# Two transformer-like blocks on one core: another order of work around dots, latent norm and copies in a selection stage, of depthwise taps, of doubled keys and of first down jobs

## The reference, cut to what matters

```
# block 1
h = rms_norm(x) * (1 + scale) + shift
glu, q, k, v, o, gates, merge = split(h @ w_in)
conv branch:  causal depthwise conv of glu, 31 taps, layer norm, pointwise product
mLSTM branch: short conv of q and k, 4 heads of 256, chunks of 64
x += g1 * (g_conv * y_conv + g_mlstm * y_mlstm) @ w_out
x += g2 * (silu(gate) * up) @ w_ffn_down
# block 2, layer a
q, c_kv, k_rope, q_idx, k_idx, w_idx, q_mem = split(rmsnorm(x) @ a_w_in)
score[t, s] = sum over 16 heads of relu(q_idx[t] . k_idx[s]) * w_idx[t]     # the indexer, heads of 64
keep the 128 highest scores of each row (top-k), attention of 8 heads over the kept
keys, with k and v from rmsnorm(c_kv) through w_uk and w_uv; cross attention to a memory
x += out @ w_out;  x += conv_glu_ffn(rmsnorm(x))                            # ffn1
# block 2, layer b
q, k, v, q_mem = split(rmsnorm(x) @ b_w_in)
banded attention, 16 query heads on 4 key heads of 64, window 128, a sink per head; memory
x += out @ w_out;  x += conv_glu_ffn(rmsnorm(x))                            # ffn2
out = rmsnorm(x)
```

## Time and profile before

| | |
|---|---|
| median of 3 executions | 2098.21 us (2096.07 to 2098.29) |
| the profiled execution | 2093.14 us |
| its span | 2091.3 us |
| granted TensorE clock | 0.999 of full speed |
| PE busy | 2058.3 us (98%) |
| DVE, ACT, POOL busy | 989.1, 885.9, 840.8 us |
| DMA | 220.15 MB, mean 105 GB/s |

### The profile page before, as it was taken

The page is one execution under the profiler, slowest core; times in us unless marked ns, Lnnn a source line. Parts: engine busy times, 40 slices in busy tenths (PEclk is TensorE's granted clock), DMA queues, the critical chain, the costliest instruction groups (busy, mean ns, idle before and its releaser), DMA issues.

```text
span 2091.3 us, 28597 instructions
## 1 busy us (share of the span) xinstructions
PE 2058.3 (98%) x10618; PEld 1735.0 (83%) x10618; DVE 989.1 (47%) x1909; ACT 885.9 (42%) x1307; POOL 840.8 (40%) x273
## 2 busy tenths in 40 slices
PE   9999999999999999999999999999999999999998
PEld 6888877788888888876878888888887688888887
DVE  4889688573411011376985344034323934431432
ACT  3355445363443122534366453233423954432332
POOL 3443432444344444443713443444443044444443
PEclk9999999999999999999999999999999999999999
DMA  9654311235233342332202433333432034324322
GB/s 370 244 183 127 102 61 61 90 98 181 67 103 92 101 118 79 97 108 66 79 24 64 113 100 89 112 102 97 143 86 74 2 96 120 101 79 122 101 73 88
DMA packets 304071, 220.15 MB, mean 105 GB/s; under 512 B 13584, under 2 KB 288144, under 8 KB 301680
## 3 DMA queue, kind: packets, MB, share of 16 engines
q1 hardware_dynamic: 293216, 195.67, 31.4%
q10 hardware_dynamic: 10768, 23.33, 3.7%
HBM read 213.48 MB, written 2.10 MB: 103 GB/s over the span
## 4 chain that ended last, share of the span: by engine, by line
PE 82%; DVE 10%; issue 4%; ACT 3%; POOL 2%; ACTq 0%; DVEq 0%; POOLq 0%
PE bank L912 68%; PE bank L1135 2%; PE bank L1347 2%; DVE bank L2287 2%; PE bank L1325 2%; DVE arena L2784 1%; PE bank L1283 1%; DVE small L2782 1%; DVE bank L2250 1%; PE bank L1334 1%; PE bank L1430 1%; PE bank L1183 1%; DVE bank L2229 1%; POOL w_split_out L2824 1%; ACT w_split L1585 1%
## 5 line engine op out<-in xcount | busy, mean ns | idle before, releaser
L912 PE MATMUL bank<-h_hi,w_split 128*128 128x512 f32 x3696 | 1118.2, 381 | 1.8 <-DVE arena L2652 1.1
L2824 POOL TENSOR_TENSOR w_split<-wslots,w_split 128x2048 fp32r<-128x2048 f32 (+3 forms) x174 | 712.8, 4097 | 987.6 <-ACT w_split L1585 549.5
L912 PEld LDWEIGHTS bank<-h_hi,w_split 128*128 128x128 f32 x3696 | 697.9, 189 | 116.5 <-issue 15.7
L912 PE MATMUL bank<-h_lo,w_split 128*128 128x512 f32 x1848 | 701.1, 379 | 0.0
L912 PEld LDWEIGHTS bank<-h_lo,w_split 128*128 128x128 f32 x1848 | 349.3, 189 | 51.1 <-issue 3.4
L912 PE MATMUL bank<-hid_hi,w_split 128*128 128x512 f32 x1056 | 315.9, 379 | 1.9 <-DVE hid_lo L2532 1.9
L1606 ACT ACTIVATE w_split<-wslots 128x2048 fp32r<-128x2048 f32 (+2 forms) x80 | 141.4, 1767 | 368.0 <-PE bank L912 368.0
L1585 ACT ACTIVATE w_split<-wslots 128x2048 fp32r<-128x2048 f32 (+3 forms) x91 | 158.7, 1744 | 298.6 <-PE bank L912 277.0
L912 PEld LDWEIGHTS bank<-hid_hi,w_split 128*128 128x128 f32 x1056 | 199.6, 189 | 31.4 <-DVE hid_lo L2532 3.2
L912 PE MATMUL bank<-hid_lo,w_split 128*128 128x512 f32 x528 | 200.1, 379 | 0.0
L2250 DVE SCALAR_TENSOR_TENSOR bank<-arena,cols,bank 128x512 f32<-128x512 f32 x240 | 161.4, 750 | 5.5 <-ACT bank L1699 4.9
(11 more groups left out here) (341 smaller groups left out, 2353.5 us busy)
## 6 DMA issues: line engine op xcount, KB each, us to landing
wslots<-in_f_w_up SPq DMA_DIRECT2D x88, 512.0 KB, 4.7
wslots<-in_w_in SPq DMA_DIRECT2D x24, 1024.0 KB, 5.4
wslots<-in_w_ffn_up SPq DMA_DIRECT2D x44, 512.0 KB, 4.6
arena<-in_w_ada ACTq DMA_DIRECT2D x8, 2048.0 KB, 9.6
wslots<-in_f_w_down SPq DMA_DIRECT2D x16, 768.0 KB, 4.9
wslots<-in_a_w_in SPq DMA_DIRECT2D x10, 1024.0 KB, 5.3
wslots<-in_f_w_down SPq DMA_DIRECT2D x16, 640.0 KB, 4.6
arena<-in_w_ada_first SPq DMA_DIRECT2D x8, 1024.0 KB, 18.7
```

The lines of the kernel that those rows point to most:

```text
L912: return nc.tensor.matmul(bank[:], w, woven(x), start=start, stop=stop)
L2824: last = nc.gpsimd.tensor_tensor(part[:, 1, cols_of], slot(p, 1, size)[:, 0, cols_of], part[:, 0, cols_of].bitcast(F32), ALU.subtract)
```

## The change

There are five places, and in all of them the computation stays as it is; only order, banks and the shape of some copies differ.

1. `CONV_TAPS`: five and five taps at steps 14 and 15 become none and ten.
2. Selection stage, PE: `turn_w_idx` moves from a_idx0 to behind product 16 of a_idx1, into bank 6, and waits for `rope_ready` 2; twelve instead of ten pairs stand in a_idx2 and a_idx3, each 7 to 8 products apart; `LATE_DOTS` 14; a_qmem holds two places of dots instead of three, and the latent's mean behind its product 22; the spread moves into a_q0, to bank 5, and a_q0 waits for the root only. ACT and DVE follow: other ranges of relus and weighted sums, ACT's split for a_qmem's successor a_q0 and the latent's squares between the last relus, and its copies of the latent's high part behind a_q0, `latent_norm` from (1, 4) to (2, 0), `memory_queries` from (1, 7) to (1, 10), and each of `ROPES_AT` one round later. POOL lowers a_q1 in one piece instead of four, and the latent's low part behind a_q2.
3. `first_downs`: the first two jobs of `ffn1_down1` and `ffn2_down1` run as tiles 0 to 8 of the first, 0 to 2 of the second, 9 of the first, 3 to 9 of the second.
4. The doubled keys: four DMAs of 64x2x512 instead of eight of 64x512, and an Exp table load on ACT moves ahead of b_q.
5. `attend` takes a table of early work instead of one function; for layer b it holds the same step at the same place.

```diff
-CONV_TAPS = (0, 0, 10, 10, 10, 10, 10, 10, 5, 5, 5, 5, 5, 5, 5, 5, 10, 0, 6, 0)
+CONV_TAPS = (0, 0, 10, 10, 10, 10, 10, 10, 5, 5, 5, 5, 5, 5, 0, 10, 10, 0, 6, 0)
...
-        ROPES_AT = {(2, 8): (0, 2), (3, 2): (2, 4), (3, 9): (4, 6), (3, 13): (6, 8)}
+        ROPES_AT = {(2, 9): (0, 2), (3, 3): (2, 4), (3, 10): (4, 6), (3, 14): (6, 8)}
...
-        DOTS_AT = {("a_idx", 2): [(i, k, k + 1) for k, i in enumerate((10, 18, 27, 38, 46))],
+        DOTS_AT = {("a_idx", 2): [(i, k, k + 1) for k, i in enumerate((9, 16, 24, 32, 40, 47))],
...
-        LATE_DOTS = 12
+        LATE_DOTS = 14
...
+            def first_downs(name, kc, rhs, waits):
+
+                p, _ = one(name, 0)
+                other, _ = one(name, 1)
+                w = {q: [w_split[q][:, part, 0:kc * P].rearrange("p (c n) -> p c n", n=P) for part in range(2)] for q in (p, other)}
+
+                def tiles(q, first, end):
+                    for c in range(first, end):
+                        if q == p:
+                            pe.wait_ge(S[waits[0]], waits[1] + c + 1)
+                        for wp, hp in ((0, 0), (0, 1), (1, 0)):
+                            last = product_of(banks[2 * q], w[q][wp][:, c, :], rhs(c, hp), c == 0 and wp + hp == 0, c == kc - 1 and wp == 1)
+                    if end == kc:
+                        last.then_inc(product_done[q], 1)
+
+                for j, (q, first, end) in enumerate(((p, 0, kc - 1), (other, 0, 3), (p, kc - 1, kc), (other, 3, kc))):
+                    if j < 2:
+                        start_split(name, j)
+                    tiles(q, first, end)
+                for i, u, q, use in pairs(pe, name, 1):
+                    pe.wait_ge(lo_ready[q], SPLITS_BEFORE[FIRST[name] + u] + i + 1)
+                    pe.wait_ge(bank_free[q], use + 1)
+                    split_job(q, kc, P, rhs, None, 1)
...
             def turn_w_idx():
-                pe.wait_ge(*emptied("a_keys", 0))
+                pe.wait_ge(S["rope_ready"], 2)
...
             def kv_spread():
                 pe.wait_ge(S["rows_inverse"], HEADS + 4)
-                spread_rows(banks[0], square[:, 0, :], P).then_inc(S["rows_spread"], 1)
+                pe.wait_ge(S["relu_used"], 2 * len(DOTS))
+                spread_rows(banks[5], square[:, 0, :], P).then_inc(S["rows_spread"], 1)
...
-                                    18: latent, 34: kv_spread})
-            pe.wait_ge(S["norm_ready"], TILES_BEFORE["kv"] + 2)
-            for j in range(4):
+                                    22: latent})
+            pe.wait_ge(S["root_ready"], NORM_NO["kv"] + 1)
+            woven_job("a_q", 0, {10: kv_spread})
+            for j in range(1, 4):
...
-                    first, end = ((0, 10), (10, 20), (20, 36))[j - 1]
+                    first, end = ((0, 12), (12, 24), (24, 40))[j - 1]
                     relu(first, first + 2)
                     split_job(slot_after(FIRST["a_idx"] + j))
                     relu(first + 2, end)
+            nc.scalar.activation(small[:, 122:123], con("eps", 1), ACT.Sqrt)
+            relu(40, 44)
             split_job(slot_after(FIRST["a_kv"]))
-            nc.scalar.activation(small[:, 122:123], con("eps", 1), ACT.Sqrt)
-            relu(36, 40)
...
-            for kv in range(4):
-                head = 64 * (kv % 2)
+            for head in (0, 64):
                 for half in (0, 64):
-                    act.dma_start(kw_heads[half:half + 64, kv, :], tile(KEYS[kv // 2])[head:head + 64, :]).then_inc(S["dup_ready"], 16)
+                    act.dma_start(kw_heads[half:half + 64, head // 64:4:2, :], key_tiles[head:head + 64, :, :]).then_inc(S["dup_ready"], 16)
...
-                    if (b, k) == (1, 4):
+                    if (b, k) == (2, 0):
                         latent_norm()
-                    if (b, k) == (1, 7):
+                    if (b, k) == (1, 10):
                         memory_queries()
...
-            lower_job("a_q", 1, 4)
-            for c in range(2):
-                pool.wait_ge(S["half_upper"], KV_HALVES + c + 1)
-                nc.gpsimd.tensor_tensor(kv_split[1][:, c, :], kv_low[:, c, :], kv_split[0][:, c, :].bitcast(F32), ALU.subtract).then_inc(S["half_lower"], 1)
+            lower_job("a_q", 1)
```

More of the change, by code:

```diff
@@ L1297, in ffn @@
                         late_product(name, f"ffn{k}")
-                    split_product(f"ffn{k}_down{half}", n, P, lambda c, part: hid[part][:, c, :], ("hid_ready", 2 + FT * k + t0), tiles=1)
+                    waits, tiles_of = ("hid_ready", 2 + FT * k + t0), lambda c, part: hid[part][:, c, :]
+                    if k and half:
+                        first_downs(f"ffn{k}_down{half}", n, tiles_of, waits)
+                    else:
+                        split_product(f"ffn{k}_down{half}", n, P, tiles_of, waits, tiles=1)
             ffn(0)
@@ L2719, in attend @@
                         weights(g - 1)
-                    if g == LAG and early:
-                        early()
+                    if early and g in early:
+                        early[g]()
                     if g > SUM_LAG and (g - SUM_LAG) % TB == 0:
```

62 lines of the change are left out of this document (35 added, 27 removed).

## The result

The changed kernel is slower: 2101.65 us median against 2096.82 for the kernel before, ratio 1.0019 (95% interval 1.0013 to 1.0026), over 18 executions of each. The prediction was 2098.1 with 0.66 on "within 0.2%", a change of −0.1; the measured time lies in its range, the measured change (about +4 by the ratio) does not go with its sum. The profiled execution took 2097.07 us (span 2095.3, mean clock 0.998), 3.9 above the one of before.

A forecast was written before the change was run, and what follows sets the result against it. TensorE, busy 98% of the span, was taken as the bound, with VectorE's chain bounding top-k. Taps −2.0, keys −1.6, down jobs +0.5 and selection stage +3.0 summed to −0.1: 2098.1 us, range 2091.5 to 2103.

The forecast's parts named there:

- Taps: At ScalarE's copy L1755: without taps ahead of VectorE's L2287, PE's 3.05 us stop shrinks; −2.0 us, bounds 0 to −3.05.
- First down jobs: PE's two 0.95 us stops for hid_lo stay, and later weight splits cost 0.25 each; +0.5 us, bounds −1.9 to +1.0.
- Doubled keys: Four key transfers land before PE arrives, removing its 1.61 us stop; −1.6 us, bounds 0 to −1.7.
- time hangs little on what moves, and I take the whole: Key transfers: eight all land in 2.4 us, so double-size ones were taken as equally quick and the whole stop as gained.
- The other bound of the same term: Key transfers: at 4.8 us to land, the last lands at 1606.8 and 0.3 us is gained.
- Selection stage: Five moves around indexer dots, top-k and masks, priced together at +3.0 us, bounds −3.7 to +8.
- Top-k's late start: Late first dots, bank waits and ScalarE's extra work before the last relus start top-k at 992.95, not 989.7: +3.3 us.
- N: Top-k: first mask goes before POOL's lowering, gaining 3.5 us, but the second loses 2.35; attention starts at +1.9.
- L: Top-k: POOL's lowering goes first, the first mask waits to 1014.7 and the second only 0.2 us; +4.1.
- with the wait for keys of a_uk growing to 3 to 5 us under cover of VectorE: In a_uk: PE waits longer for keys but still ends before VectorE's last mask, 1062.8 against 1063.3 in N.
- if PE and no longer VectorE ends last ahead of the attention: Ahead of attention: a sign, named beforehand, that the forecast of VectorE ending last was wrong.
- Rival S: Top-k: masks lock behind POOL's 4.5 us lowerings, two of three hit; stage +8.6, total +5.5, 2103.7 us; chance 0.10.

The follow-up runs named there:

- uv_split_back: The changed kernel with ScalarE's split of a_uv's weights back in its old place, ahead of a_q3's transfers; 2098.67 us, ratio 1.0013 to the kernel before.
- keys_eight: The changed kernel with eight key transfers of 64x512 again, the table load staying at its new place; 2099.78 us, ratio 1.0016 to the kernel before.
- after_load: The changed kernel with SP's load of a_kv's weights held until a_idx0's rotated rows have landed; 2100.07 us, ratio 1.0019 to the kernel before.
- old_stage: The kernel before with the change's taps, down jobs and four key transfers, keeping its own selection stage; 2094.61 us, ratio 0.9990.
- taps_only: The kernel before with only the taps moved (the one line CONV_TAPS); 2093.00 us, ratio 0.9984.
- stage_turn: taps_only with turn_w_idx and ScalarE's copy of its result moved as in the change; 2095.37 us, ratio 0.9996 to the kernel before.
- stage_turn_load: stage_turn with SP's load of a_kv's weights held until a_idx0's rotated rows have landed; 2094.49 us, ratio 0.9995 to the kernel before.

## Why the prediction was wrong, by its own steps

The sum said −0.1 and the profiled executions differ by +3.9. Of the 4.0 between them the keys are 1.8 and the selection stage 2.0. The forecast time of 2098.1 comes nearer to the measured one than the forecast change does, and that is luck: it stands on the median of three executions of the kernel before, 2098.21, and the median of 18 is 2096.82.

- **Taps, −2.0: right.** 1.6 to 2.1 by the traces, 2.9 at equal clock.
- **First down jobs, +0.5: right in size.** +0.6 measured. The stops stayed, behind the bank, and the late lowering costs up to 0.2, as forecast; the rest, 0.15 at each stop (0.95 became 1.10), was in no term.
- **Doubled keys, −1.6: wrong, +0.2 measured.** The step that failed is "time hangs little on what moves, and I take the whole". Equal landing times of eight transfers of one size say nothing about another size. The other bound of the same term (4.8 us to land, 0.3 gained) was near what happened.
- **Selection stage, +3.0: +5.0 in the profiled execution.** Top-k's late start was right in size (+3.3 forecast, +3.15 measured) and for the dots in mechanism. For the transposes the mechanism was half: their stop, but also SP's megabyte among the small transfers, which the count by engines had not in it, since it gave each transfer a fixed time. Of N and L it was L (+4.1), and the middle of the two, which the sum took, was no case that could happen. The step that failed is "with the wait for keys of a_uk growing to 3 to 5 us under cover of VectorE". The stop was 5.05, near the forecast's upper end, but a stretch at the lower clock followed it, which costs 1.7; TensorE would have had 0.45 us in hand and came 1.25 too late for VectorE's step behind the last mask. It took both: uv_split_back has the stretch behind a stop of 2.50 and no such wait. The prediction had named this as a sign of being wrong ("if PE and no longer VectorE ends last ahead of the attention").
- **What no term held: the clock of the other executions.** The mean clock of the runs is 0.9976 before (in the later comparisons) and 0.9963 after, which by the slope is 1.85 us, on top of 2.85 at equal clock. The sum is 4.7, the difference of the medians 4.8. That the change lowers the clock by this much is not shown: keys_eight and after_load, which have the same long stop, ran at 0.9973 and 0.9969.

By the profile: −1.9 (taps) + 5.0 (stage) + 0.2 (keys) + 0.6 (down jobs) = +3.9, as the spans differ. Without the wait of 1.25 it would have been +2.7, which the prediction's own case L would have given with the right price for the keys (+1.0, with +0.2 in place of −1.6: +2.8). Rival S's total of +5.5 came near, by another way: one mask was held, not two. What stays open is why some stops are followed by a stretch at the lower clock and others not.

## What to carry to other kernels

A stop of the bounding engine is not worth only its length: behind stops of 1.6 to 5 us TensorE ran slowly for 3.4 us or more in some executions of this case, so stops hidden under another engine's work still have to be counted, and so does the cover that is left. When an edit frees an engine earlier, look at what that frees in turn (here a weight slot and with it a 1 MB load) and what is under way on the queues then; and when taking one delay away gives nothing, try it together with the next late thing before dropping the theory. A large POOL instruction near a one-instruction VectorE step on the bounding chain is worth cutting into pieces, all those that can meet it at once: in the kernel before, one alone only moved the wait.

## What the runs showed of the hardware

- In the 20 profiled executions the lower clock came inside the kernel in stretches of 3.4 us, single or double, in 16 of them. All began between 0.8 us ahead of the end of a stop of TensorE of 1.6 us or more and 12 us behind it, most within 2. Behind the kernel's first 20 us there are 53 such stops in the 20 executions, and 23 were followed by a stretch: all three of 5.05 us, but not the one of 3.05. Each stretch of 3.4 us cost 1.7 where TensorE or what waits for it was the bound (reciprocal at 85.03 in old_stage, 83.33 in taps_only). The mean clock of a run goes with three quarters of the variance of the kernel before's times: runs at 0.999 had a median of 2094.7 and those at 0.995 of 2099.8.
- Transfers of 256 KB within SBUF, four in a row, landed 3.2 to 4.9 us after their issue (changed kernel), eight of half that size 2.4 (before). Whether the size or the form of the copy makes the difference is open.
- Four small transfers took 5.0 to 5.5 us while a 1 MB load was starting on another queue (changed kernel: issue of the last at 916.2, VectorE released at 921.2; stage_turn: 917.2 and 922.67). With the load held back they took under 2.5 (stage_turn_load: issue of the last at 916.5, SP, which waits for them, issues at 918.84).
